# Low halves of weight slabs made ahead of sums of squares, and of the turned roots, in a 256-token two-block transformer kernel

## The reference, cut to what matters

```python
def rms_norm(x, g):
    y = xf * lax.rsqrt(jnp.mean(xf * xf, axis=-1, keepdims=True) + EPS)
    return (y * g.astype(jnp.float32)).astype(x.dtype)

for l in range(DEPTH):                       # DEPTH = 2
    a = hybrid_mixer(rms_norm(x, pre_mix_g[l]), ..., w_in[l], ...)
    x = x + rms_norm(a, post_mix_g[l])
    c = memory_cross_attention(rms_norm(x, pre_xattn_g[l]), rms_norm(mem, mem_g[l]), ...)
    x = x + rms_norm(c, post_xattn_g[l])
    hdn = jnp.square(jax.nn.relu(rms_norm(x, pre_mlp_g[l]) @ w_up[l]))
    x = x + rms_norm(hdn @ w_down[l], post_mlp_g[l])
return second_block(x, ...)
```

## Time and profile before

| what | us |
|---|---|
| median of 3 timed executions | 1268.82 (1264.76 to 1275.01) |
| the profiled execution, its own time | 1267.79 |
| its span, first to last instruction | 1266.0 |
| TensorE busy | 1220.7 (96%) |
| VectorE busy | 831.5 (66%) |
| ScalarE busy | 670.5 (53%) |
| GpSimd busy | 48.1 (4%) |

### The profile page before, as it was taken

One profiled execution on the slowest core, in us unless ns is written; L12 is line 12 of the kernel. 1 busy time (PEld: TensorE's weight loads), 2 busy tenths in 40 slices (PEclk: granted clock), 3 DMA queues, 4 the chain that ended last, 5 costly groups with the idle time before them and its releaser, 6 DMA issues.

```text
span 1266.0 us, 23291 instructions
## 1 busy us (share of the span) xinstructions
PE 1220.7 (96%) x10107; PEld 1190.5 (94%) x10107; DVE 831.5 (66%) x988; ACT 670.5 (53%) x967; POOL 48.1 (4%) x41
## 2 busy tenths in 40 slices
PE   5999999999999999999999999999899999999998
PEld 5989998989999999999898999999799998999998
DVE  5688549577664587854867676448677866676442
ACT  5466545465543356654655664335476754565331
POOL 3000000000000000000000000100300100000000
PEclk9999999999999999999999999999989999999999
DMA  7734544336655543454434665764442453366652
GB/s 243 227 115 135 167 165 146 114 117 216 210 190 190 175 134 105 134 172 161 135 103 137 217 209 177 213 214 142 124 156 67 136 164 99 125 211 200 197 181 88
DMA packets 195571, 202.89 MB, mean 160 GB/s; under 512 B 5716, under 2 KB 191847, under 8 KB 195471
## 3 DMA queue, kind: packets, MB, share of 16 engines
q1 hardware_dynamic: 192704, 194.82, 48.1%
q0 software_dynamic: 2464, 5.99, 1.6%
q10 hardware_dynamic: 303, 0.61, 0.2%
HBM read 200.33 MB, written 3.16 MB: 161 GB/s over the span
## 4 chain that ended last, share of the span: by engine, by line
PE 83%; DVE 8%; ACT 4%; DMA 2%; issue 2%; POOL 0%; DVEq 0%; ACTq 0%; POOLq 0%
PE bank L593 14%; PE bank L595 14%; PE bank L594 14%; PE bank L2464 7%; PE bank L2466 7%; PE bank L2468 7%; DVE w_lo L553 3%; ACT w_hi L543 2%; PE bank L2374 2%; PE bank L2358 2%; PE bank L657 2%; PE bank L658 1%; PE bank L659 1%; DVE x_t L1523 1%; DMA raw<-in_w_in_dram 1%
## 5 line engine op out<-in xcount | busy, mean ns | idle before, releaser
L553 DVE TENSOR_TENSOR w_lo<-raw,w_hi 128x2048 fp32r<-128x2048 f32 (+7 forms) x210 | 424.6, 2031 | 262.9 <-ACT w_hi L543 262.6
L543 ACT ACTIVATE w_hi<-raw 128x2048 fp32r<-128x2048 f32 (+7 forms) x210 | 355.6, 1705 | 327.7 <-PE bank L2468 112.2
L593 PE MATMUL bank<-act_hi,w_hi 128*128 128x256 f32 (+1 forms) x1104 | 307.6, 279 | 5.4 <-DVE w_lo L553 4.1
L595 PE MATMUL bank<-act_hi,w_lo 128*128 128x256 f32 (+1 forms) x1104 | 305.7, 277 | 0.0
L594 PE MATMUL bank<-act_lo,w_hi 128*128 128x256 f32 (+1 forms) x1104 | 305.7, 277 | 0.0
L593 PEld LDWEIGHTS bank<-act_hi,w_hi 128*128 128x128 f32 (+1 forms) x1104 | 206.6, 187 | 7.4 <-issue 5.6
L595 PEld LDWEIGHTS bank<-act_hi,w_lo 128*128 128x128 f32 (+1 forms) x1104 | 207.2, 188 | 0.1
L594 PEld LDWEIGHTS bank<-act_lo,w_hi 128*128 128x128 f32 (+1 forms) x1104 | 206.7, 187 | 0.2
L2464 PE MATMUL bank<-h_hi,w_hi 128*128 128x256 f32 x736 | 203.6, 277 | 0.0
L2468 PE MATMUL bank<-h_hi,w_lo 128*128 128x256 f32 x736 | 203.5, 276 | 0.0
L2466 PE MATMUL bank<-h_lo,w_hi 128*128 128x256 f32 x736 | 203.5, 276 | 0.0
(11 more groups left out here) (412 smaller groups left out, 2177.6 us busy)
## 6 DMA issues: line engine op xcount, KB each, us to landing
raw<-in_w_up_dram SPq DMA_DIRECT2D x32, 1024.0 KB, 5.4
raw<-in_w_down_dram SPq DMA_DIRECT2D x32, 1024.0 KB, 5.2
raw<-in_w_ff_dram SPq DMA_DIRECT2D x32, 1024.0 KB, 5.4
raw<-in_w_in_dram SPq DMA_DIRECT2D x23, 1024.0 KB, 5.3
raw<-in_w_xk_dram SPq DMA_DIRECT2D x8, 1024.0 KB, 5.4
raw<-in_w_xv_dram SPq DMA_DIRECT2D x8, 1024.0 KB, 5.3
raw<-in_w_mix_out_dram SPq DMA_DIRECT2D x8, 1024.0 KB, 5.3
raw<-in_w_xq_dram SPq DMA_DIRECT2D x8, 1024.0 KB, 5.3
```

Source lines behind the costliest of these rows:

```text
L543: ins = act.activation(d, r, ACT.Copy)
L553: ins = dve.tensor_tensor(d, r, h.bitcast(F32), ALU.subtract)
L593: pe.matmul(o, stat_hi, mov_hi, start=first, stop=False)
L595: return pe.matmul(o, stat_lo, mov_hi, start=False, stop=last)
```

## The change

At the MLP entry of both layers, and at the entry of layer 1, the high half of the third slab (34, and 66, which is slab 2) is made on ScalarE right after the fifth tile of x. Its low half is made on VectorE right after the last tile's low half; the additions of the squares (`fold_eps`, `fold_pair` 1 to 3, `fold_tiles`) all come after it. TensorE runs that slab before stat 5 (stat 0); this new order of stat 0 and slab 2 is in the list for layer 0 too, where nothing else of this part changes. At the end of layer 1 (66 then belongs to the second block) ScalarE's order changes, VectorE's doesn't. In the MLP slab 35's halves come ahead of the root, and `hidden_up` starts with slab 36. In both layers slab 7's low half comes ahead of `token_roots`.

```diff
 TE_ORDER = (
-    [("pair", 0), ("stat", 0), ("slab", 2), ("slab", 3), ("slab", 4), ("slab", 5),
+    [("pair", 0), ("slab", 2), ("stat", 0), ("slab", 3), ("slab", 4), ("slab", 5),
...
-     ("stat", 4), ("pair", 32), ("stat", 5)]
-    + [("slab", s) for s in range(34, 64)] + [("stat", 6)])
+     ("stat", 4), ("pair", 32), ("slab", 34), ("stat", 5)]
+    + [("slab", s) for s in range(35, 64)] + [("stat", 6)])
...
-            def scaled_hi(layer, first, src, dst, gain, n=8, src_ready=None, square=None, gains=g_cur, k0=0, k1=None):
+            def scaled_hi(layer, first, src, dst, gain, n=8, src_ready=None, square=None, gains=g_cur, k0=0, k1=None, split=None):
...
+                    if split is not None and k == 4:
+                        split_hi(act, layer, split)
...
                 scaled_hi(layer, 24, x_t, act_hi, G_PRE_MLP, square=4,
-                          src_ready=lambda k: act.wait_ge(sig["x_new"], value("x_new", layer, 8 + k + 1)))
-                split_hi(act, layer, 34)
+                          src_ready=lambda k: act.wait_ge(sig["x_new"], value("x_new", layer, 8 + k + 1)), split=34)
+                split_hi(act, layer, 35)
                 x_root_of(layer, 5, "stat5", T)
                 for b in range(16):
-                    split_hi(act, layer, 35 + b)
+                    if b < 15:
+                        split_hi(act, layer, 36 + b)
                     squared_up(layer, b)
...
                 scaled_hi(layer, 32, x_t, act_hi, 0, square=6, gains=g_next,
-                          src_ready=lambda k: act.wait_ge(sig["x_new"], value("x_new", layer, 16 + k + 1)))
-                split_hi(act, layer, 66)
+                          src_ready=lambda k: act.wait_ge(sig["x_new"], value("x_new", layer, 16 + k + 1)), split=66)
...
                     if k:
                         rest(layer, "act_lo", next_first + k, x_t, next_gain, act_hi, act_lo, next_gains)
-                    if k == 4:
+                    if k == 4 and not later:
                         fold_eps(layer, norm)
-                    if k == 5:
+                    if k == 5 and not later:
                         fold_pair(layer, norm, 1)
-                fold_pair(layer, norm, 2)
+                if not later:
+                    fold_pair(layer, norm, 2)
                 rest(layer, "act_lo", next_first + 8, x_t, next_gain, act_hi, act_lo, next_gains)
+                if later:
+                    split_lo(dve, layer, later)
+                    fold_eps(layer, norm)
+                    fold_pair(layer, norm, 1)
+                    fold_pair(layer, norm, 2)
                 fold_pair(layer, norm, 3)
                 fold_tiles(layer, norm)
...
-            def hidden_up(layer, used, split):
+            def hidden_up(layer, used, splits):
...
-                        split_lo(dve, layer, split + b)
+                        if b < len(splits):
+                            split_lo(dve, layer, splits[b])
...
+                split_lo(dve, layer, 7)
                 token_roots(layer)
-                split_lo(dve, layer, 7)
...
-                residual(layer, 4, 1, 4, G_POST_X, 24, G_PRE_MLP)
-                split_lo(dve, layer, 34)
+                residual(layer, 4, 1, 4, G_POST_X, 24, G_PRE_MLP, later=34)
+                split_lo(dve, layer, 35)
                 inverse_root(layer, 5, rstd[:, 0:T], root[:, 0:T])
-                hidden_up(layer, 33, 35)
+                hidden_up(layer, 33, range(36, 51))
...
-                residual(layer, 6, 2, 8, G_POST_MLP, 32, 0, g_next)
                 if layer + 1 < DEPTH:
+                    residual(layer, 6, 2, 8, G_POST_MLP, 32, 0, g_next, later=66)
                     layer_gains(layer + 1)
-                split_lo(dve, layer, 66)
+                else:
+                    residual(layer, 6, 2, 8, G_POST_MLP, 32, 0, g_next)
+                    split_lo(dve, layer, 66)
```

More of the change, by code:

```diff
@@ L1501, in o_rest, with residual @@
                     .then_inc(sig["o_lo"], 1)
-            def residual(layer, stat, norm, a_first, gain, next_first, next_gain, next_gains=g_cur):
+            def residual(layer, stat, norm, a_first, gain, next_first, next_gain, next_gains=g_cur, later=None):
                 factor = branch_root if norm or layer == 0 else down_inverse
@@ L2210, in _ @@
             inverse_root(DEPTH, 2, rstd[:, 0:T], root[:, 0:T])
-            hidden_up(DEPTH, 28, 30)
+            hidden_up(DEPTH, 28, range(30, 46))
             for b in range(4):
```

## The result

The change made the kernel slower: 1276.76 us in the median (1272.94 to 1281.05, 8 runs) against 1266.11 for the kernel before on the same chip (1264.23 to 1275.01, 8 runs). The ratio is 1.0075, 95% interval 1.0059 to 1.009. Forecast were 1264.4 and a range of 1260 to 1270. The profiled executions have spans of 1275.1 and 1266.0: 9.1 us to explain. Granted clock over the whole span: 0.994 (before 0.992).

The account below looks back on a forecast made before the run. TensorE was taken as the bound, so only its waits could be won. Layer 0 +0.2, MLPs -2.3 and layer 1 -1.25 gave -3.4 us, from 1267.8 to 1264.4 us; range 1260 to 1270.

Parts of the forecast that it names:

- the first one: Whole kernel: TensorE is busy 1220.7 of 1266.0 us, so only its waits, 45 us together, can be won.
- MLP's third slab: Slab 34 in both MLPs: ready 0.8 us early, its low-half wait goes, gaining 0.95 us in layer 0, 1.35 in layer 1.
- Third slab of layer 1: Slab 2 at layer 1's entry: its 1.21 us wait mostly passes to slab 3, gain 0.1, between 0 and 1.4.
- Layer 0's order: Layer 0's entry: stat 0 behind slab 2 delays the memory's copies, slab 3 waits 2.5 us, a loss of 1.3 us.
- the second turning: Attention after slab 7: TensorE waits for the second probabilities, giving back 0.4 us in layer 0, 0.45 in layer 1.
- the rival of 0.20: Slab 3 of layer 0: the clock falls at the new wait, 1.7 us more, 1266.1; chance 0.20.
- Slab 7: Slab 7 follows `kpe` without its low-half wait: gain 1.53 us in layer 0, 1.60 in layer 1.
- the prediction's own rule of 0.16 more than the row says: TensorE's timeline: each wait removed is worth 0.16 us more than its row shows.
- the rival that nothing of this gain is kept: Attention: VectorE and ScalarE set the pace, so slab 7's net 2.25 us are lost, 1266.7; chance 0.12.
- the six waits of the earlier trace: Argument against losing slab 7's gain: of six low-half waits, 9.1 us together, none lies in the attention.
- The clock: New 2.5 us wait at layer 0's slab 3: a fall would cost 1.7 us, not counted because full slabs stand either side.
- Sum: Layer 0 +0.2, MLPs -2.3, layer 1 -1.25, together -3.4 us; the second block unchanged.

Follow-up runs that it names:

- experiment 5: Kernel before with only the MLP's part of the change (slab 34 ahead of stat 5), layer entries and slab 7 as before: 1275.95 us, ratio 1.0075.
- 1: Changed kernel with the six unused float32r products ahead of slab 35, behind stat 5, instead of ahead of slab 34: 1265.91 us, ratio 0.9983.
- experiment 6: Changed kernel with one unused float32r product ahead of slab 35 and none ahead of slab 34: 1262.91 us, ratio 0.9965.
- 8: Kernel before with one unused float32 product ahead of slab 48, mid-stream in the MLP of both layers: 1273.86 us, ratio 1.0053.
- experiment 4: Kernel before with only slab 7's low half moved ahead of the copy of the turned roots, both layers: 1263.68 us, ratio 0.9967.
- experiment 10: Kernel before with 1, 2, 3, 4, 5, 7 float32 products ahead of slabs 36 to 46 (even), one float32r ahead of each next slab: 1286.83 us, one execution.
- version 14: Kernel before with the MLP's and slab 7's parts, one unused product ahead of slab 35 replacing six ahead of slab 34: 1264.8 us, ratio 0.9984.
- experiment 3: Changed kernel with layer 0 back in its old order, stat 0 ahead of slab 2: 1275.05 us, ratio 1.0052.
- 7: Changed kernel with six unused float32 products ahead of slab 35 in place of the six float32r ones ahead of slab 34: 1268.18 us, ratio 1.0021.

## Why the prediction was wrong

**The step that failed is the first one: "So only what makes TensorE wait can be won".** The sum was one of waits and of instructions' durations, and a stream of products was costed at 0.118 each wherever it stood. The forecast said of stat 5 only when the sum, the root and the inverse would be there behind it. It never asked what stat 5 does to the products behind it, since in a timeline an instruction moved within one engine's list seems to cost its own 0.43 us at either place. The term that was missing is 2 x 1389 x 4.5 ns = +12.5 us, shown by experiment 5 (there alone), 1 and 6 (gone with unused products between) and 8 (made by one float32 product). What makes two paces stays open. No rival held it either: each had a wait or the clock for its reason, and the range was drawn for the scatter of medians alone.

It could have been read. Five slabs of layer 1 took 5.67 us each, which is 118 ns a product; the 100 us window in the MLP shows 885 products, 113 ns. Two values of the same thing, at one clock, in one trace, are a question.

Point by point:
- **MLP's third slab: right.** The low half of slab 34 starts at once behind the last tile's, and the pair covers it. VectorE's timeline of the kernel after, against the earlier trace rows:

```profile
272.05 2.28 DVE L553 TENSOR_TENSOR w_lo<-raw,w_hi 128x2048 fp32r<-128x2048 f32 x1
274.25 0.42 DVE L1410 TENSOR_TENSOR qk_dil<-qk_dil,rstd_c 128x256 f32<-128x256 f32 x1
```

  It is ready at 274.3 and TensorE comes at 275.37: 1.0 to spare, forecast 0.8. Nothing waits at slab 36, as worked out (0.17 to spare).
- **Third slab of layer 1: right.** The wait of 1.21 went to slab 3 as 0.94 (forecast 1.1); layer 1 gained 1.16 (forecast 1.25). That sum came out in part by luck: the pair at its start ran at 117.8 ns in place of 113.5, 0.4 us that the forecast didn't have.
- **Layer 0's order: right, with its rival.** The wait is 2.51 (forecast 2.5). The clock fell behind it, the rival of 0.20, +1.7 us. Of the 3.5 by which this stretch missed the forecast that leaves 1.8. Followed product by product, the pace of the 192 products of slabs 3 to 6 is 0.6 to 0.7 of it (125.8 ns each against 113.4, clock and pace together 2.4 us), the pace of 156 products of the attention from 113 to 134 us (117 ns against 113) another 0.6, a turning in the cross-attention that now waits (224 us) 0.3, and the second turning and the wait at slab 3 are 0.2 each over their forecasts.
- **Slab 7: right in its waits.** Both are gone, and the second turning waits for 0.43 in either layer (forecast 0.4 and 0.45). By the prediction's own rule of 0.16 more than the row says, that is 0.6 of time, so the part is worth 2.0 where it stands and not 2.25. Measured alone it gave 0.0033, 4.2 us (2.1 to 6.3 by the interval), of which experiment 4's profile gives slab 7 about 1.6; so the rival that nothing of this gain is kept fails, and a part is lost. Its argument had a misreading: the six waits of the earlier trace rows are L593's alone, without the two on the unused products, and two of the other three stand in the cross-attention, on slab 26 (1.26 at 205.77 us, 1.67 at 622.18).
- **The clock.** Against a fall the prediction had waits of 1.2 to 1.4 us and the one of 2.16, with the clock full behind them. It overlooked the wait of 1.47 us at 905.56 in the same trace, behind which the clock fell (window below).
- **Sum.** Of the span: -3.4 as forecast, +1.7 for the clock, +12.5 for the pace is +10.8, against 9.1 between the two profiles and 10.6 between the medians. The prediction also held that a measurement here can't tell less than 1% from no change; eight executions of each kernel told 0.75% with an interval of 0.15 on either side.

## What to carry to other kernels

Before an instruction is moved within the list of the engine that is the bound, read how many instructions of the main stream that engine makes in equal stretches of the trace (the windows view gives it in one row), and not only where it waits: 100% busy says nothing of the pace. Where a product of another data type stands directly ahead of a long stream, try one more product of the stream's own kind between them (in experiment 10 it helped behind one float32 product and not behind two or four), and judge it by the range of many executions, as one profile shows one draw. And a change in parts is best timed in parts: here one part gave 0.3% and another took 0.75.

## What the runs showed of the hardware

- Streams of float32r products (128 x 128 weights, 256 columns) ran with 113.3 or 117.8 ns from start to start, at the 2.4 GHz level, and kept to one value for up to 1437 products. The Trainium skill, page "TensorE: Matmul & The Clock Gate" (Part 2, Back-to-back issue gap), gives 262 cycles or 109 ns as the isolated gap for 256 columns and says that in a real stream weight load and product together set the spacing. The trace agrees that the isolated figure isn't the spacing of a stream: both values lie above it.
- The clock's fall isn't a matter of the wait's length alone. In the kernel before it fell behind a wait of 1.47 us and was at its 1.2 GHz level again from 930 to 936 us, with TensorE busy throughout and no wait over 0.26 us since the one of 2.16 at 913.51, behind which it had stayed full:

```profile
905.56:910.56 5.00, 5.00 (x29) 0.67 0.16 20
...
930.00:936.00 6.00, 6.00 (x30) 0.50 0.67 217
```

- The same holds between kernels. Near 24 us and near 45 us of the span TensorE waits in every kernel. With layer 0 in its old order, in 12 of 13 profiles the stretch behind exactly one of the two waits ran at a mean of 0.66 or near it; in version 14, the fastest, behind neither. Its wait of 1.80 us left the clock at 1.00, where 1.81 us in experiment 3 was followed by the fall. In experiment 6 the early wait of 2.61 us left it at 1.00, where 2.61 us had cost 1.7 us before. With layer 0 in the new order (after, 1, 6, 7) it fell behind the later wait in all four profiles, and in two behind the early one too. TensorE's windows behind both waits, in slab 7 alone (waits 2.64 and 1.43), then in version 14 (1.15 and 1.80):

```profile
24.00:29.00 5.00, 5.00 (x32) 0.66 1.05 341
45.00:50.00 5.00, 4.25 (x37) 1.00 0.79 240
```

```profile
24.00:29.00 5.00, 5.00 (x46) 1.00 1.05 342
45.00:50.00 5.00, 5.00 (x47) 1.00 0.66 210
```

  The prediction's rule from the same page (Part 1), that where the change between slow and fast falls differs between runs of one kernel, would fit that. No run here shows it as such, for each kernel has one profile.
